# Two transformer blocks on one core: the down product's second half in the up product's banks, and the final norm ahead of the overflow branch

## What is computed

```
def rmsnorm_2(x, w):   # final norm, also ahead of every part
    return x * rsqrt(mean(x * x, axis=-1) + EPS) * w

def swiglu_2(h, w_gate, w_up, w_down):          # width 1024 -> 2816 -> 1024
    a = einsum("bsd,df->bsf", h, w_gate)
    u = einsum("bsd,df->bsf", h, w_up)
    return einsum("bsf,fd->bsd", silu(a) * u, w_down)

...
    x = x + moe_swiglu(h, router_w, w_gate, w_up, w_down)   # top 2 of 8 experts
    return rmsnorm_2(x, norm_final_w)
```

## Time and profile before

| | us |
|---|---|
| median of three runs | 2709.48 |
| lowest, highest | 2709.4, 2711.61 |
| the profiled execution's own time | 2712.34 |
| its span (first to last instruction) | 2710.4 |
| PE busy | 2523.1 (93%) |
| DVE busy | 1757.6 (65%) |
| ACT busy | 1475.7 (54%) |

### The profile page before, as it was taken

One profiled execution on the slowest core, in us unless ns is written; L12 is line 12 of the kernel. 1 busy time (PEld: TensorE's weight loads), 2 busy tenths in 40 slices (PEclk: granted clock), 3 DMA queues, 4 the chain that ended last, 5 costly groups with the idle time before them and its releaser, 6 DMA issues.

```text
span 2710.4 us, 42798 instructions
## 1 busy us (share of the span) xinstructions
PE 2523.1 (93%) x17242; PEld 2230.9 (82%) x17242; DVE 1757.6 (65%) x2364; ACT 1475.7 (54%) x1892; POOL 27.9 (1%) x85
## 2 busy tenths in 40 slices
PE   4998899999999889999889999897999999999997
PEld 2875689999997689988689999686888888888885
DVE  3445856455455765555555546556888988888886
ACT  3235545444343655355554435554777777777775
POOL 0000000000000000010000001000000000000000
PEclk8998999999999999999999999898999999999998
DMA  7224535445442634445134555231999999999994
GB/s 279 102 100 156 187 109 186 179 172 181 173 158 92 251 146 177 186 153 177 50 122 162 182 179 167 76 140 63 340 356 352 350 356 353 352 354 351 354 354 176
DMA packets 81578, 565.99 MB, mean 209 GB/s; under 512 B 9264, under 2 KB 12592, under 8 KB 13552
## 3 DMA queue, kind: packets, MB, share of 16 engines
q1 hardware_dynamic: 80096, 559.95, 55.3%
q0 software_dynamic: 1296, 3.38, 0.5%
HBM read 559.92 MB, written 1.05 MB: 207 GB/s over the span
## 4 chain that ended last, share of the span: by engine, by line
PE 84%; DVE 8%; ACT 5%; issue 2%; DMA 0%; SPq 0%; PEldq 0%; DVEq 0%; ACTq 0%
PE psum L232 82%; DVE ring_lo L226 2%; ACT ring_hi L223 1%; PE psum L641 1%; DVE hT L718 1%; PE psum L1859 1%; DVE hT L1221 1%; DVE hT L429 1%; ACT hT L682 1%; ACT Z L690 0%; ACT L415 0%; DMA ring<-in_stream 0%; DVE Z L1195 0%; DVE Z L1194 0%; DVE h_lo L439 0%
## 5 line engine op out<-in xcount | busy, mean ns | idle before, releaser
L226 DVE TENSOR_TENSOR ring_lo<-ring,ring_hi 128x2048 fp32r<-128x2048 f32 x479 | 1096.9, 2291 | 472.2 <-ACT ring_hi L223 469.1
L223 ACT ACTIVATE ring_hi<-ring 128x2048 fp32r<-128x2048 f32 x479 | 916.1, 1914 | 390.0 <-PE psum L232 387.8
L232 PE MATMUL psum<-a_hi,ring_hi 128*128 128x256 f32 (+1 forms) x2448 | 733.4, 300 | 59.8 <-DVE h_lo L437 20.1
L232 PE MATMUL psum<-a_hi,ring_lo 128*128 128x256 f32 (+1 forms) x2448 | 727.5, 297 | 0.0
L232 PE MATMUL psum<-h_lo,ring_hi 128*128 128x256 f32 (+1 forms) x2128 | 630.2, 296 | 0.0
L232 PEld LDWEIGHTS psum<-a_hi,ring_hi 128*128 128x128 f32 x2448 | 477.1, 195 | 78.5 <-issue 44.0
L232 PE MATMUL psum<-ring_hi,a_hi 128*128 128x512 f32 (+1 forms) x1680 | 521.0, 378 | 5.9 <-DVE h_lo L437 3.7
L232 PEld LDWEIGHTS psum<-a_hi,ring_lo 128*128 128x128 f32 x2448 | 476.6, 195 | 10.4
L232 PEld LDWEIGHTS psum<-h_lo,ring_hi 128*128 128x128 f32 x2128 | 415.6, 195 | 7.6
L232 PEld LDWEIGHTS psum<-ring_hi,a_hi 128*128 128x128 f32 x1680 | 313.5, 189 | 58.1 <-issue 4.1
L232 PE MATMUL psum<-ring_lo,a_hi 128*128 128x512 f32 (+1 forms) x976 | 353.2, 362 | 0.0
(11 more groups left out here) (256 smaller groups left out, 2382.7 us busy)
## 6 DMA issues: line engine op xcount, KB each, us to landing
ring<-in_stream SPq DMA_DIRECT2D x529, 1024.0 KB, 4.8
mixT<-mixT POOLq DMA_DIRECT2D x32, 71.0 KB, 5.5
cst<-in_constants SPq DMA_DIRECT2D x1, 1216.0 KB, 15.1
xT<-in_xT SPq DMA_DIRECT2D x1, 1024.0 KB, 9.5
xT<-in_ctxT SPq DMA_DIRECT2D x1, 1024.0 KB, 11.8
xT<-in_memT POOLq DMA_DIRECT2D x1, 1024.0 KB, 6.0
out_y<-hT SPq DMA_DIRECT2D x1, 1024.0 KB, 4.8
Z<-in_level_masks SPq DMA_DIRECT2D x1, 448.0 KB, 15.4
```

The costliest lines, as they stand in the source:

```text
L223: e.activation(hi, raw, ACT.Copy).then_inc(sem("piece_rounded"), 1)
L226: e.tensor_tensor(lo, raw, hi.bitcast(F32), ALU.subtract).then_inc(sem("piece_split"), 1)
L232: ins = pe.matmul(*args, **kw)
```

## The change

**Banks.** In run 1 the up product now uses banks 4 to 7, in the other runs 0 to 3 as before (`ups`). The first half of the down product takes the four banks that the up product of its run doesn't use, and the second half those of the up product (`downs`). The wait on `down_added` is gone from PE. A norm's mean after run 2 or 3 is in bank 4, after run 1 still in bank 0.

**Final norm.** `pe_last_norm`, `act_last_norm` and `dve_last_norm` stand right behind the experts, ahead of the meeting and the branch, and a second time inside the branch. ACT squares two tiles at a time, each pair once DVE has added it. The mean is in bank 2. The second meeting after the branch and the drain ahead of the store are gone. SP stores the output in two halves, each once DVE has scaled its four tiles.

```diff
+        rs_last = hT[:, 0, T:2 * T]
+        def pe_last_norm(pe, pre):
             for k in range(KT):
+                if k % 2 == 0:
+                    pe.wait_ge(sem("last_squared"), 4 * (pre == "o") + k // 2 + 1)
+                mm(pe, bank[2][:, 0:T], const("mean"), hT[:, k, 0:T], start=k == 0, stop=k == KT - 1,
+                   last_of="last_mean" if k == KT - 1 else None)
+        def act_last_norm(act, pre):
+            act.preload_act_table_set("natural_log")
+            for b in range(4):
+                act.wait_ge(sem(pre + "_x_added"), N_EXP * 4 + b + 1)
+                act.activation(hT[:, 2 * b:2 * b + 2, 0:T], xT[:, 2 * b:2 * b + 2, 0:T], ACT.Square)\
+                   .then_inc(sem("last_squared"), 1)
+            act.wait_ge(sem("last_mean"), 1 + (pre == "o"))
+            link(act, act.activation(rs_last, bank[2][:, 0:T], ACT.Ln, bias=EPS))
+            act.activation(rs_last, rs_last, ACT.Exp, scale=-0.5).then_inc(sem("last_root"), 1)
+        def dve_last_norm(dve, pre):
+            dve.wait_ge(sem("last_root"), 1 + (pre == "o"))
+            for k in range(KT):
+                ins = dve.scalar_tensor_tensor(hT[:, k, 0:T], xT[:, k, 0:T], v("final2", 0, k, k + 1), rs_last,
+                                               ALU.mult, ALU.mult)
+                if k % 4 == 3:
+                    ins.then_inc(sem("y_ready"), 1)
...
+        def ups(run):
+            return bank[4:8] if run == 1 else bank[0:4]
+        def downs(run, half):
+            return bank[0:4] if (run == 1) != (half == 1) else bank[4:8]
...
-                    if f == 0 and half == 1:
-                        pe.wait_ge(sem("down_added"), run * 8 + d + 1)
                     for i, (wp, ap) in enumerate(THREE):
                         last = f == FT - 1 and i == 2
-                        mm(pe, bank[4 + d][:, 0:T], w[wp][:, (q % 4) * 512 + d * P:(q % 4) * 512 + (d + 1) * P],
+                        mm(pe, downs(run, half)[d][:, 0:T], w[wp][:, (q % 4) * 512 + d * P:(q % 4) * 512 + (d + 1) * P],
...
+                sp.wait_ge(sem("y_ready"), 4)
             sp.nop()
-            sp.wait_ge(sem("y_ready"), 1)
-            sp.dma_start(y_out, hT[:, :, 0:T]).then_inc(sem("y_stored"), 16)
-            sp.wait_ge(sem("y_stored"), 16)
+            for half in range(2):
+                sp.wait_ge(sem("y_ready"), half + 1)
+                tiles = slice(4 * half, 4 * half + 4)
+                sp.dma_start(y_out[:, tiles, :], hT[:, tiles, 0:T]).then_inc(sem("y_stored"), 16)
+            sp.wait_ge(sem("y_stored"), 32)
...
                     pe_experts(pe, "e", 0)
+                    pe_last_norm(pe, "e")
                     phase_end(pe)
                     with pe.If(pe.value_load(overflow[0:1, 0:1], min_val=0, max_val=1) > 0):
                         pe_experts(pe, "o", N_EXP // 2)
+                        pe_last_norm(pe, "o")
                     pe.nop()
-                    phase_end(pe)
-            pe_norm(pe, 0, T)
```

More of the change, by code:

```diff
@@ L503, in up @@
                     last = k == KT - 1 and i == 2
-                    mm(pe, bank[2 * (f % 2) + half][:, 0:T], w[wp][:, k * 256 + half * P:k * 256 + (half + 1) * P],
+                    mm(pe, ups(run)[2 * (f % 2) + half][:, 0:T], w[wp][:, k * 256 + half * P:k * 256 + (half + 1) * P],
                        h(ap, k, off, off + T), start=k == 0 and i == 0, stop=last,
@@ L546, in act_ffn @@
                         act.wait_ge(sem("hidden_full"), run * FT + f - 1)
-                    act.activation(mixT[:, f % 2, 0:T], bank[2 * (f % 2)][:, 0:T], ACT.Silu)\
+                    act.activation(mixT[:, f % 2, 0:T], ups(run)[2 * (f % 2)][:, 0:T], ACT.Silu)\
                        .then_inc(sem("silu"), 1)
@@ L567, in dve_ffn @@
                     dve.wait_ge(sem("silu"), run * FT + f + 1)
-                    dve.tensor_tensor(hid(f, 1, Z), mixT[:, f % 2, 0:T], bank[2 * (f % 2) + 1][:, 0:T], ALU.mult)\
+                    dve.tensor_tensor(hid(f, 1, Z), mixT[:, f % 2, 0:T], ups(run)[2 * (f % 2) + 1][:, 0:T], ALU.mult)\
                        .then_inc(sem("hidden_full"), 1)
@@ L584, in dve_ffn @@
                     dve.wait_ge(sem("down"), run * 8 + q + 1)
-                    ps, x = bank[4 + q % 4][:, 0:T], xT[:, q, off:off + T]
+                    ps, x = downs(run, half)[q % 4][:, 0:T], xT[:, q, off:off + T]
                     dve.scalar_tensor_tensor(x, ps, gains(q), x, ALU.mult, ALU.add).then_inc(sem("down_added"), 1)
@@ L2018, in act_two_norms @@
             await_next(act, "mean_of_normed")
-            act.activation(rs_two[:, 0:T], bank[0][:, 0:T], ACT.Ln, bias=EPS)
+            act.activation(rs_two[:, 0:T], bank[4][:, 0:T], ACT.Ln, bias=EPS)
             link(act, act.activation(rs_two[:, T:2 * T], rs_two[:, T:2 * T], ACT.Ln, bias=EPS * EPS))
@@ L2026, in dve_two_norms @@
             await_next(dve, "two_means")
-            link(dve, dve.tensor_scalar(rs_two[:, T:2 * T], bank[0][:, 0:T], EPS, None, ALU.mult))
-            dve.tensor_tensor(rs_two[:, T:2 * T], rs_two[:, T:2 * T], bank[0][:, T:2 * T], ALU.add)\
+            link(dve, dve.tensor_scalar(rs_two[:, T:2 * T], bank[4][:, 0:T], EPS, None, ALU.mult))
+            dve.tensor_tensor(rs_two[:, T:2 * T], rs_two[:, T:2 * T], bank[4][:, T:2 * T], ALU.add)\
                .then_inc(sem("mean_of_normed"), 1)
@@ L2155, in _ @@
                 else:
-                    pe_mean(pe, 0, (3, 4, 5, 6, 7), 0, 2 * T, "two_means")
+                    pe_mean(pe, 4, (3, 4, 5, 6, 7), 0, 2 * T, "two_means")
             for layer in range(DEPTH):
@@ L2174, in _ @@
                     pe_ffn(pe, 3)
-                    pe_mean(pe, 0, (3, 4, 5, 6, 7), 0, T)
+                    pe_mean(pe, 4, (3, 4, 5, 6, 7), 0, T)
                 else:
@@ L2223, in _ @@
                 else:
-                    act_rms(act, 0, 0, T)
+                    act_rms(act, 4, 0, T)
                     act_apply(act, [b2_segment("norm_mix", 1)])
@@ L2251, in _ @@
                     act_experts(act, "e", 0)
+                    act_last_norm(act, "e")
                     phase_end(act)
@@ L2254, in _ @@
                         act_experts(act, "o", N_EXP // 2)
+                        act_last_norm(act, "o")
                     act.nop()
-                    phase_end(act)
-            act_last_norm(act)
         @block.vector
@@ L2328, in _ @@
                     dve_experts(dve, "e", 0)
+                    dve_last_norm(dve, "e")
                     phase_end(dve)
@@ L2334, in _ @@
                         dve_experts(dve, "o", N_EXP // 2)
+                        dve_last_norm(dve, "o")
                     dve.nop()
-                    phase_end(dve)
-            dve_last_norm(dve)
-            dve.drain().then_inc(sem("y_ready"), 1)
         @block.gpsimd
```

7 lines of the change are left out of this document (removed).

## The result

| | before, us | after, us |
|---|---|---|
| median | 2710.55 (4 runs) | 2688.07 (4 runs) |
| lowest, highest | 2709.4, 2711.99 | 2683.57, 2690.81 |
| profiled execution: own time | 2712.34 | 2687.88 |
| its span | 2710.4 | 2686.0 |
| PE busy | 2523.1 (93%) | 2511.2 (93%) |

The ratio is 0.9915 with a 95% interval of 0.9904 to 0.9927. The forecast was 2690.0 within 2684.5 to 2695. The work of DVE is unchanged. Of the 24.4 us between the spans, 11.9 us are busy time of PE, which has 17242 matmuls in both kernels and ran fewer of them at the low clock; the rest is waiting.

A forecast was written before the change was run, and what follows sets the result against it. PE, on 84% of the last-ending chain, was taken as the bound, with waits at half boundaries and the end. Gains of 12.3 and 9.35 us, 21.7 together, led to 2690.0 us, range 2684.5 to 2695.

The forecast's parts named there:

- Edit 1, 12.3 us: Down product's half boundaries: PE no longer waits for DVE's residual add, four boundaries return to 5.76 us pace, gaining 12.3 us.
- The rival that the wait is only replaced: Half boundaries: PE finds its next piece unsplit or bank reads hold matmuls up; no gain there, 2700 us; chance 0.1.
- The split of the term: Half boundaries: 9.2 us plain waiting at four places, 3.1 us from the clock falling to 1.2 GHz in two.
- Edit 2, up to DVE's last product: Final norm moved ahead of the branch: the chain after DVE's last add ends 9.5 us earlier.
- The mean: Final norm on PE: 16 records take 3.6 us at full clock, 6.63 before; a slow clock would lose 3.2 us.
- The end: After DVE's last product: PE's branch ends last, 5.35 us later, 0.15 us later than the store did before.
- a branch that grows from running side by side: Program end: sign of being wrong, PE's branch taking longer than about 3.8 us when run beside the store.
- The store: Program end: the output's second half takes 3.5 us, bounded by 2.4 and 4.8 us, ending before PE's branch.
- The short branch: Program end: rival that PE's branch is short and the store ends last, 1.4 us more gained, 2688.6 us; chance 0.12.
- The sum: Whole kernel: 12.3 us at the half boundaries plus 9.35 us at the program's end, 21.7 us in all.
- The rival that the clock moves: Later stretches of the kernel: clock falls change places, giving 2693 to 2695 us or 2686 us; chance 0.2, half either way.
- The two ways to the median: Whole kernel: median 2690.9 us if the faster runs had no clock falls at the boundaries, 2687.8 if they had; 2690.0 taken.

The follow-up runs named there:

- e3: The changed kernel with PE's wait on `down_added` put back ahead of the down product's second half, banks as in the change; 2701.98 us.
- e1: The kernel before with only the new banks, moved means and removed wait, the end of the program as before; 2697.0 us, ratio 0.9947.
- e5: The changed kernel without the meeting, the flag and the branch behind the final norm; 2681.44 us in a single run.
- e8: The changed kernel run once more, unaltered, as reference for later kernels; 2688.11 us.
- e6: The changed kernel with the flag loaded ahead of the final norm and the meeting only inside the branch; 2684.38 us.
- e4: The changed kernel with one store of the whole output in place of two halves; 2691.93 us in a single run.
- e2: The changed kernel with its bank and wait edits undone, so only the new final norm and two stores remain; 2702.43 us, ratio 0.9961.

## Why the prediction was right, step by step

- **Edit 1, 12.3 us.** Right in the profiled execution: every boundary went to 5.76 us, no other wait came up, and no piece came late. The rival that the wait is only replaced fell with the idle time of 0.0. The split of the term, 9.2 us of waiting and 3.1 us of clock, is borne out by e3: with the wait back, the waiting part returned (9.4 us) and the clock's part only once.
- **Edit 2, up to DVE's last product.** I said 8.3 us from A to D and it was 8.17. The mean was to take 3.6 us at full clock and took 3.62, and in e1, which keeps the old end, 6.72. The squares lie beside the adds and the mean.
- **The end.** The right thing ends last, the branch on PE, and e5 shows it. Its size was off: the span ends 5.95 us after D, not 5.35. The step that failed is the sentence that the branch's time "would then not depend on what comes before it". It grew from 3.79 to 4.28 us, and the flag's load ahead of it from 0.49 to 0.79, since the stores now run beside them. The prediction had named just this, a branch that grows from running side by side, as a sign of being wrong, and it came, too small to move the sum. These two terms are more than the 0.6 us that were missing. The store, taken at 3.5 us between two bounds, landed in 3.1.
- **The short branch.** It didn't happen in any kernel with the branch; PE's took 3.4 us or more. What spoke for it, ACT's 45 ns, was misread: ACT's sequencer shows nothing for 2.4 us behind that record in the kernel before, and for 3.5 us in the change (2681.3 to its drain at 2684.8). ACT waits as well, only the record doesn't hold the wait.
- **The sum.** 12.3 + 8.8 = 21.1 us of the 24.4 us between the two spans. The other 3.3 us lie elsewhere, in stretches in which no instruction differs. At the first boundary the changed kernel is 0.75 us later (542.10 against 541.35), at run 2's it has lost 1.65 us of its lead (1142.46 against 1147.79, a lead of 5.33 where 6.98 had been gained), by run 3's it has won 2.99 us back, and from there to A another 2.64 us. Multiplied out over stretches of 2.5 us, the time that PE lost at the low clock was 64.0 us before and 55.8 after; 3.1 of the difference is edit 1's, 2.9 the mean's, and the remaining 2.2 us most of the 3.3. The rival that the clock moves was thus present, with the lucky sign in that execution.
- **The two ways to the median.** I took 2690.0 between 2687.8 (the falls at the boundaries belong to all runs) and 2690.9. The median came to 2688.07, on the side of the first. e3 shows both kinds of boundary, so this was not a firm ground for choosing. In time, edit 1 alone gave 14.4 us (10.6 to 18.2) where its term is 12.3, and the change as repeated in e8 24.4 us where the forecast medians are 19.5 apart. That the median fell within 2 us of the forecast is in part luck.

## What to carry to other kernels

Where an accumulation is done in halves, look for banks that an earlier product has left: the second half can start in them while the first is still being read, and the wait costs more than its own length where the clock falls behind it. Put whatever has to be waited for anyway, such as a branch that skips much code, beside work that doesn't need it, and load its condition early; ahead of the end of a program, its time is all exposed. And count the table loads between two functions that always follow each other: one set for Ln and Exp in all norms took 11.5 us of waiting off PE's path here, about half of the whole change, and 18.7 us off the median.

## What was not expected of the hardware

- PE's branch over the skipped code took 3.44, 3.79, 4.28 and 6.34 us, the first two (e6, before) with no store in flight, the third (the change) beside the rest of a half, the last (e4) beside a whole one; on ACT the instruction itself took 45 ns in all four, and in the kernel before, the change and e4 its wait lies as a gap of 2.4, 3.5 and 3.7 us behind the record.
- The branch's wait goes with packets on the instruction queues (five in the kernel before, 0.05 MB), and PE's comes only once the store's packets are nearly through: 3.7 us after the branch began in e4, 0.9 us without a store.
- The flag's load took 0.49 us on PE in the kernel before and in e4, and 0.79 us in the change, where the first half's store was in flight.
- A stall of PE of 2.0 us at the same place was followed by a clock of 1.2 GHz for some 3 us in some executions (before, e2) and not in another (e3). The same kernel's runs spread over 1.5 to 8.5 us. Such falls are a part of that, not all of it: the fastest of the change's four runs (2683.57) has a mean granted clock of 0.968, lower than the 0.970 of the first two. So an edit at the end of the program worth 1 to 3 us is to be read in the rows and not in the time.
